# A recurrent branch kept in PSUM, its gates behind every third tile, gelus at the end, weights ahead of squares

## What is computed

```python
h = rmsnorm_2(x, norm_mix_g[l])
proj = h @ w_in[l]
u_x, u_g, q, k, v, g_lru, g_att = jnp.split(proj, split_idx, axis=-1)
c = causal_depthwise_conv(u_x, conv_w[l], conv_b[l])          # 4 taps
# rg_lru, blocks of 64 channels:
r = sigmoid(xb @ w_r + b_r);  i = sigmoid(xb @ w_i + b_i)
log_a = -8 * r * softplus(-lam)
a = exp(log_a);  mult = sqrt(-expm1(2 * log_a));  u = mult * (i * c)
h_t = a_t * h_{t-1} + u_t                                     # scan over 512 positions
y_lru = h * gelu(u_g)
```

## Time and profile before

| what | us |
| --- | --- |
| three runs | 1833.65, 1832.16, 1828.87 (median 1832.16) |
| profiled execution | 1828.52, of which span 1825.8 |
| TensorE busy over the span | 1713.2 (94%) |
| VectorE, ScalarE, GpSimd busy | 714.1, 603.6, 565.9 |

### The profile page before, as it was taken

The page is one execution under the profiler, slowest core; times in us unless marked ns, Lnnn a source line. Parts: engine busy times, 40 slices in busy tenths (PEclk is TensorE's granted clock), DMA queues, the critical chain, the costliest instruction groups (busy, mean ns, idle before and its releaser), DMA issues.

```text
span 1825.8 us, 20365 instructions
## 1 busy us (share of the span) xinstructions
PE 1713.2 (94%) x8350; PEld 1196.7 (66%) x8350; DVE 714.1 (39%) x1058; ACT 603.6 (33%) x787; POOL 565.9 (31%) x263
## 2 busy tenths in 40 slices
PE   7889796999999999978799999999999999999995
PEld 5667574344444444346588977777778788888882
DVE  6565635233333333358831013322344322222335
ACT  5565443111100110045521255554334332232331
POOL 3231133222102220031244434443443444444440
PEclk9989998999999999999999999999999999999997
DMA  5121172799999999942122111112232222223201
GB/s 204 58 70 47 35 291 92 321 420 421 421 421 421 421 421 421 419 170 75 46 92 93 47 47 47 47 47 92 92 139 92 93 93 92 93 93 110 75 35 46
DMA packets 75068, 308.56 MB, mean 169 GB/s; under 512 B 3008, under 2 KB 4448, under 8 KB 50272
## 3 DMA queue, kind: packets, MB, share of 16 engines
q1 hardware_dynamic: 74704, 306.18, 42.9%
q0 software_dynamic: 272, 1.05, 0.2%
HBM read 305.12 MB, written 2.10 MB: 168 GB/s over the span
## 4 chain that ended last, share of the span: by engine, by line
PE 82%; DVE 10%; ACT 4%; issue 3%; POOL 1%; DMA 0%; DVEq 0%; SPq 0%; ACTq 0%
PE ps L854 39%; PE ps L1186 12%; PE ps L896 7%; PE ps L1210 6%; PE ps L1140 4%; PE ps L852 3%; PE ps L1333 2%; PE ps L1155 1%; ACT sb_slot L1400 1%; PE ps L1156 1%; PE ps L1318 1%; PE ps L1354 1%; DVE sb_R L2311 1%; POOL sb_w_parts L794 1%; ACT sb_R L1400 1%
## 5 line engine op out<-in xcount | busy, mean ns | idle before, releaser
L794 POOL TENSOR_TENSOR sb_w_parts<-sb_slot,sb_w_parts 128x2048 fp32r<-128x2048 f32 x59 | 274.3, 4650 | 414.1 <-ACT sb_w_parts L1400 414.1
L854 PE MATMUL ps<-sb_h_high,sb_w_parts 128*128 128x512 f32 x1120 | 274.3, 397 | 16.9 <-POOL sb_w_parts L794 8.7
L854 PEld LDWEIGHTS ps<-sb_h_high,sb_w_parts 128*128 128x128 f32 x1120 | 211.9, 190 | 68.4 <-issue 12.5
L1186 PE MATMUL ps<-sb_slot,sb_hT 128*64 128x512 f32 x768 | 171.2, 595 | 0.0
L1400 ACT ACTIVATE sb_w_parts<-sb_slot 128x2048 fp32r<-128x2048 f32 x59 | 112.6, 1910 | 172.4 <-PE ps L854 172.4
L854 PE MATMUL ps<-sb_hidden_high,sb_w_parts 128*128 128x512 f32 x704 | 166.9, 392 | 1.9 <-ACT sb_hidden_high L1400 1.9
L854 PEld LDWEIGHTS ps<-sb_hidden_high,sb_w_parts 128*128 128x128 f32 x704 | 133.3, 189 | 30.1 <-ACT sb_hidden_high L1400 2.3
L758 POOL TENSOR_TENSOR sb_tile_parts<-sb_slot,sb_tile_parts 128x1024 fp32r<-128x1024 f32 x32 | 79.4, 2484 | 200.2 <-ACT sb_tile_parts L1400 200.2
L854 PE MATMUL ps<-sb_h_low,sb_w_parts 128*128 128x512 f32 x560 | 138.8, 391 | 0.0
L1186 PEld LDWEIGHTS ps<-sb_slot,sb_hT 128*64 128x64 f32 x768 | 53.6, 137 | 106.2 <-issue 106.2
L854 PEld LDWEIGHTS ps<-sb_h_low,sb_w_parts 128*128 128x128 f32 x560 | 105.9, 189 | 22.1
(11 more groups left out here) (312 smaller groups left out, 2658.7 us busy)
## 6 DMA issues: line engine op xcount, KB each, us to landing
sb_slot<-w_up SPq DMA_DIRECT2D x24, 2048.0 KB, 15.6
sb_slot<-w_gate SPq DMA_DIRECT2D x24, 2048.0 KB, 15.5
sb_slot<-w_down SPq DMA_DIRECT2D x21, 2048.0 KB, 16.4
sb_slot<-w_in SPq DMA_DIRECT2D x14, 2048.0 KB, 8.1
sb_R<-w_down SPq DMA_DIRECT2D x11, 2048.0 KB, 15.9
sb_slot<-tiles SPq DMA_DIRECT2D x32, 512.0 KB, 3.4
sb_R<-w_gate SPq DMA_DIRECT2D x8, 2048.0 KB, 15.3
sb_R<-w_up SPq DMA_DIRECT2D x8, 2048.0 KB, 15.9
```

Source lines behind the costliest of these rows:

```text
L794: nc.gpsimd.tensor_tensor(low, raw_part(g), high.bitcast(F32), ALU.subtract).then_inc(w_low, 1)
L854: ins = nc.tensor.matmul(o, w[:, k, at:at + P], h[:, k, :], start=first, stop=last)
L1186: ins = nc.tensor.matmul(ps_[b * CAP:(b + 1) * CAP, bank0, :], xgT[:, k, at:at + CAP], w[:, b, kk * 512:(kk + 1) * 512], start=(k == 0), s ...
```

## The change

It has five parts, all in the tiles ux, ug and the first two of q2.

1. The eight squares leave the step `feed` and become a step `squares`, which stands behind the weights of ux 2 and 3; the sum over partitions stands behind ux 2 instead of ux 1.
2. The gate products of a pair stand behind tiles 5, 8, 11 and 14 (ux and ug counted together), so each pair waits for tiles done earlier; the weights of the next items stand ahead of the gates' arithmetic.
3. ux is multiplied by `rstd` in place in PSUM and the convolution reads it there; its result for all eight tiles has a place of its own in SBUF (`lc`). Sigmoids, the third function (Exp of minus 16, in place of a squaring), and both products with i are written to PSUM in place; the scan reads its input from PSUM.
4. ug is evicted only; for tiles 0 to 5 it takes the place of `lc`. One Gelu covers six tiles and one the other two, at q2 0; two products follow at q2 1.
5. The row sums move behind ug 7.

The diff, cut:

```diff
@@ plan()
+        if base in ("ux", "ug") and first + (KD if base == "ug" else 0) in (6, 12):
+            step("lru_in", (first + (KD if base == "ug" else 0)) // 3 - 2)
+        if (base, first) == ("ux", 0):
+            step("squares")
...
-                pair = n // 2 - 1 + (4 if base == "ug" else 0)
-                if 0 <= pair < 4:
-                    if n % 2 == 0:
-                        for m in (2 * pair, 2 * pair + 1):
-                            job("lru_gate", "r", m)
-                            job("lru_gate", "i", m)
...
+                j = n + (KD if base == "ug" else 0)
+                if j in (5, 8, 11, 14):
+                    pair = (j - 5) // 3
+                    for m in (2 * pair, 2 * pair + 1):
+                        job("lru_gate", "r", m)
+                        job("lru_gate", "i", m)
+                    if j % 2 == 0:
+                        step("lru_in", pair)
+                if j == 15:
+                    step("row_norm")
+                if j in (6, 9, 12, 15):
+                    step("lru", (j - 6) // 3)
+            if base == "q2" and n < 2:
+                step(("gelu", "gated")[n])
@@ build(), TensorE
-                    if pending and arg in (("ux", 1), ("up", 1), ("pg", 1)):
+                    if pending and arg in (("ux", 2), ("up", 1), ("pg", 1)):
...
-                    pe.wait_ge(conv_done, n + 1)
+                    taken(pe, ("proj", "ux", n))
@@ build(), ScalarE
+                elif kind == "lru_in":
...
+                    for m in (2 * g, 2 * g + 1):
+                        for which, b_ in (("r", "b_rgate_2"), ("i", "b_igate_2")):
+                            st_ = ("lru_gate", which, m)
+                            finished(act, st_)
+                            fn(bank(st_), bank(st_), ACT.Sigmoid, bias=G(b_, m)).then_inc(in_gate, 1)
+                    if g:
+                        taken(act, ("lru_gate", "i", 2 * g - 1))
+                    act.wait_ge(in_gate, 4 * g + 4)
+                    for m in (2 * g, 2 * g + 1):
+                        r_ = bank(("lru_gate", "r", m))
+                        fn(la[:, m % 2, :], r_, ACT.Exp, scale=nsp8[:, m:m + 1])
+                        link(fn(lt[:, m % 2, :], r_, ACT.Tanh, scale=sp8[:, m:m + 1]))
+                        fn(r_, r_, ACT.Exp, scale=nsp16[:, m:m + 1]).then_inc(lru_exp, 1)
...
+                elif kind == "gelu":
+                    for gel, n in ((lc[:, 0:6, :], 5), (late_gel, 7)):
+                        taken(act, ("proj", "ug", n))
+                        fn(gel, gel, ACT.Gelu_apprx_tanh).then_inc(ug_done, 1)
@@ build(), VectorE
+                        link(v.tensor_tensor(o, o, rstd, ALU.mult))
+                        link(v.tensor_scalar(c_, o, G("conv_w_2", 24 + n), G("conv_b_2", n), ALU.mult, ALU.add))
+                        for tap in (2, 1, 0):
+                            late = 3 - tap
+                            ins = v.scalar_tensor_tensor(out=c_[:, late:S], in0=o[:, 0:S - late], scalar=G("conv_w_2", 8 * tap + n),
+                                                         in1=c_[:, late:S], op0=ALU.mult, op1=ALU.add)
...
+                        dve.wait_ge(lru_exp, m + 1)
+                        ins = v.scalar_tensor_tensor(out=lt[:, m % 2, :], in0=bank(("lru_gate", "r", m)), scalar=1.0, in1=lt[:, m % 2, :],
+                                                     op0=ALU.add, op1=ALU.mult)
+                        frees(ins, ("lru_gate", "r", m))
...
+                        frees(v.tensor_tensor_scan(yl[:, m, :], la[:, m % 2, :], bank(i_), 0.0, ALU.mult, ALU.add), i_)
+                elif kind == "gated":
+                    taken(dve, ("lru_gate", "i", KD - 1))
+                    for lo, hi, gel in ((0, 6, lc[:, 0:6, :]), (6, KD, late_gel)):
+                        dve.wait_ge(ug_done, 1 + lo // 6)
+                        v.tensor_tensor(yl[:, lo:hi, :], yl[:, lo:hi, :], gel, ALU.mult).then_inc(yl_done, hi - lo)
```

More of the change, by code:

```diff
@@ L1531, in _ @@
                         square(FED[s_], k)
-                    elif k == KD - 1:
-                        for j in range(KD):
-                            square(2, j)
+                elif kind == "squares":
+                    for j in range(KD):
+                        square(2, j)
                 elif kind == "split":
@@ L1930, in _ @@
                         add_square(FED[s_], k)
[L1931 to L1935 removed]
+                elif kind == "squares":
+                    for j in range(KD):
+                        add_square(2, j)
                 elif kind == "row_norm":
```

95 lines of the change are left out of this document (33 added, 62 removed).

## The result

The changed kernel takes 1802.14 us (median of 4 runs, 1801.17 to 1804.21) against 1830.63 (median of 4, 1828.87 to 1833.65): 0.9841 of the time, 95% interval 0.9826 to 0.9857. That is 1.6% less, 28.5 us by the medians. The prediction was 1803.7 with a gain of 28.5. The profiled execution took 1802.86, of which 1800.0 is its span; before these were 1828.52 and 1825.8.

A forecast was written before the change was run, and what follows sets the result against it. TensorE bounds the kernel and waits inside the stage for VectorE. 102.9 work plus 2.3 waits plus 0.4 make 105.6 us against 134.1, a gain of 28.5; from median 1832.16 that gives 1803.7 us, forecast 1799 to 1807.

The forecast's parts named there:

- What bounds: Stage from first ux tile to q2: TensorE bounds but waits for VectorE; waits and what follows them 31.2 of 134.1 us.
- The work in the sum: TensorE's own work in the stage: 102.9 us, with 0.4 more for the high parts behind the norm's sum.
- Weights ahead: Weights of ux 2, 3 ahead of the squares: h_low held about 4.5 us, TensorE waits 0.7 and 1.6, together 2.3.
- Convolution: VectorE's work on one ux tile, read from PSUM: 3.8 us, six tiles done at 844.6.
- Banks: Gates hold PSUM banks until the pair's scans; pair 1's gates have 1.1 us margin, in-place operations taken as 0.69.
- rival 1: PSUM dearer: in-place or linked operations cost 0.2 to 0.5 us more; time 1804.5 to 1808, up to 1810; chance 0.09.
- rival 2: GpSimd still holds VectorE despite PSUM operands: 15.5 us in pair 0's path, 1 to 2 later; time 1820; chance 0.04.
- rival 4: Slower, banks bind: in-place operations dearer by x cost 31x - 9.1; x must be 1.4 us; time 1838; chance 0.02.
- Gelus: Two gelus (about 2.8 and 1.1 us) and two products hidden beside q2, with 3 us to spare.
- Rival 3: Given back later: last pair, row sums and gelus delay q2 2, 3 parts; 3 to 8 us, 1807 to 1812; chance 0.07.
- DMA queues: GpSimd's DMA and SyncE's waits unchanged; first panel used up 12 us earlier, no load late before or after.
- The rule on PSUM's fixed latency: VectorE from PSUM: 120 fixed cycles against 58; 2.8 us for 43 operations ahead of pair 0's scans, time 1805; not used.

The follow-up runs named there:

- no_hold: Changed kernel, but GpSimd's first low part waits until h_low is through and the squares pass through PSUM bank 7: 1802.41 us.
- second_tile: Changed kernel with the gates placed as before, behind every second tile (ux 2, 4, 6 and ug 0), PSUM kept: 1818.98 us.
- all_sbuf: Changed kernel with both the convolution and the gates' arithmetic reading from SBUF instead of PSUM: 1814.57 us.
- slow_pairs: Changed kernel with one needless VectorE RECIPROCAL ahead of the products of pairs 0, 1 and 2: 1807.63 us.
- slow_pairs2: Changed kernel with two needless VectorE RECIPROCALs ahead of the products of pairs 0, 1 and 2: 1809.99 us.
- conv_sbuf: Changed kernel, but ux is multiplied by rstd into SBUF and the convolution reads it there: 1816.57 us.
- pair_sbuf: Changed kernel, but the sigmoids write to SBUF and the pair's arithmetic and scans read there; convolution stays in PSUM: 1807.03 us.

## Why the prediction was right, step by step

**What bounds.** That TensorE bounds and that the stage's loss was its waits holds: the stage without a wait is 102.97 (no_hold). The work in the sum was 102.9 and 0.4, 103.3 together. Two terms are off inside it: the norm's sum was put at the 1.1 of its busy time and takes 0.45 from its start to the next (819.22 to 819.67), and the second tile behind the sum takes 0.3 more than usual for its high parts (4.08 in no_hold, 4.12 in the changed kernel), which the prediction leaves out.

The prediction puts all waits down to VectorE's chain. The largest of them, 8.13 us before 906.75, ends with ScalarE, as the kernel before shows in order of time:

```profile
891.07 0.63 ACT L1400 ACTIVATE sb_R<-sb_R 128x512 f32<-128x512 f32 x1 [5.62 <-DVE sb_R L1792]
...
904.76 1.89 ACT L1400 ACTIVATE sb_w_parts<-sb_slot 128x2048 fp32r<-128x2048 f32 x1
```

TensorE starts ug 4 when the high weight parts are ready, at 904.76 + 1.89 = 906.65. ScalarE reaches them last in a queue that starts with the gelu of ug 0 at 891.07, held up by the scans of pair 2 (6.69 us where two take 2.33 unheld), and goes on with pair 3's functions, a second gelu and table loads. An estimate from these rows is 4.4 us for the held scans and 3.9 for the two gelus with the table loads that they add (891.07 to 893.01, and 895.45 to 898.69 less one load of 1.28), 8.3 together for a wait of 8.13. The wait is gone in second_tile, which has the old spacing, and in all_sbuf, which has the holds, so neither the new spacing nor PSUM was needed to remove it. Both of these have the gelus at the end.

**Weights ahead.** The waits were put at 0.7 and 1.6 us, 2.3 together. The rows show 0.17 and about 0.6 more inside the stretched low parts, then 1.26; the difference to no_hold is 105.25 - 102.97 = 2.28. The stretch of h_low was 9.75 - 5.38 = 4.4, "about 4.5" in the prediction.

**Convolution.** A ux tile was put at 3.8 us, and starts of tiles are 3.81 apart. This is two small errors that cancel: TENSOR_SCALAR from PSUM takes 0.81, where I took 0.69 from a TENSOR_TENSOR because the only row had 128 columns, and the three multiply-adds are followed by the next operation 2.24 us after their start (828.33 to 830.57), where I had 3 x 0.75 and a gap for each.

**Banks.** The room ahead of pair 1's gates was 1.1 and is 1.0, by slow_pairs and slow_pairs2. The bounds for an operation in place in PSUM were 0.64 and 1.22; it takes 0.69 to 0.70, the value taken. Scans from PSUM take about 1.2 with GpSimd busy. So rivals 1, 2 and 4 fall: there is no surcharge x to multiply. Without the room, slow_pairs shows, 2.2 us of wait would have cost 4.2; the prediction has that only in rival 1 (1.6 for the clock) and leaves it out of rivals 2 and 4. conv_sbuf shows a second bank that binds, that of ux 3 for ux 6, which the prediction doesn't name.

**Gelus.** Hidden, as said, and with more room than said, about 4 us for 3. The first gated product was held by GpSimd as forecast: the two took 8.91 us, for the 5.5 that the prediction has for them unheld. The evictions of q2 behind them waited in VectorE's queue until 928.75, and no product of TensorE waited for them. Rival 3 didn't happen in the changed kernel; pair_sbuf shows it happening once the scans are held.

**DMA queues.** None appears among TensorE's waits in the stage, as said.

**The sum.** 105.6 for a stage that took 105.25. From the medians the gain came out as 28.5, equal to the forecast; since the runs of one kernel spread over several us, and the stage of the kernel before took 134.13 in one execution and 135.90 in another (a gain of 28.9 or 30.7), agreement that close is luck.

**How the gain is made up.** Undoing one part costs, in the stage: the cadence 13.0, the places in PSUM 8.2 (and some 5 behind it: 3.03 of waiting and the slow products that follow), weights ahead of squares 5.0. These sum to 26.2, near the 28.9; but they overlap, since the convolution in SBUF alone costs 14.2 and with the pair's arithmetic in SBUF 8.2, so no exact share can be given, and that the sum comes near is no proof. What the moved gelus give was not measured: no run puts them back, though half of the largest wait before is theirs by the estimate above. The sum over partitions and the row sums, moved too, have no run either.

**The rule on PSUM's fixed latency.** On reads alone the prediction set aside the 120 against 58 cycles of the Trainium skill, "VectorE: DVE Perf Modes", section "The TRN2 errata — SBUF-src ops pay a fixed extra latency per instruction". The in-place products, at 0.69 to 0.70, agree with the rows and not with it. The 43 operations of the prediction's estimate count pair 0's two scans too; ahead of them stand 41. What does cost more from PSUM is one form, TENSOR_SCALAR, by 0.26 us.
